# Output projection: one 64-row tile's high and low activations share one stationary tile of 128 columns, and that tile moves from ninth to fifth place

## What is computed

```python
ya = rms_norm(h.astype(dt), g_a) * jax.nn.silu(za)        # first half, 1024 channels
...
yb = rms_norm(ob.astype(dt), g_b) * jax.nn.silu(zb)       # second half, 1024 channels
y = jnp.concatenate([ya, yb], axis=-1) @ w_out            # w_out: 2048 x 1024
x_out = x + gate[:, None] * y
...
y_prompt = rms_norm(xp, g_final)
y_sample = rms_norm(xs, g_final)
```

## Time and profile before

| | us |
|---|---|
| median of 3 runs (lowest, highest) | 1128.11 (1127.08, 1128.51) |
| profiled execution, its own time | 1130.15 |
| its span in the trace | 1128.3 |
| PE busy in the span | 1039.0 (92%) |
| DVE / ACT / POOL busy | 864.4 / 494.7 / 392.2 |
| mean granted TensorE clock | 0.973 |

### The profile page before, as it was taken

One profiled execution on the slowest core, in us unless ns is written; L12 is line 12 of the kernel. 1 busy time (PEld: TensorE's weight loads), 2 busy tenths in 40 slices (PEclk: granted clock), 3 DMA queues, 4 the chain that ended last, 5 costly groups with the idle time before them and its releaser, 6 DMA issues.

```text
span 1128.3 us, 16568 instructions
## 1 busy us (share of the span) xinstructions
PE 1039.0 (92%) x5914; PEld 931.5 (83%) x5914; DVE 864.4 (77%) x1643; ACT 494.7 (44%) x827; POOL 392.2 (35%) x247
## 2 busy tenths in 40 slices
PE   5989888999989998989899996899999999999996
PEld 3679666999989998989899995778878878888873
DVE  1578899999998899999999996677667656444344
ACT  4442565211223676765556324556555534111111
POOL 0223665221112444554545571233331332212120
PEclk9989999999999998989999998999999999999998
DMA  9613010232341022222113632243322336132221
GB/s 298 191 43 80 6 40 1 77 115 77 97 135 47 19 80 80 80 80 74 48 39 97 212 105 71 72 108 94 95 57 66 94 94 232 55 114 94 84 66 56
DMA packets 128281, 100.78 MB, mean 89 GB/s; under 512 B 12177, under 2 KB 119201, under 8 KB 128225
## 3 DMA queue, kind: packets, MB, share of 16 engines
q1 hardware_dynamic: 128224, 100.04, 30.2%
HBM read 74.04 MB, written 25.99 MB: 89 GB/s over the span
## 4 chain that ended last, share of the span: by engine, by line
PE 55%; DVE 25%; issue 14%; ACT 4%; DMA 1%; SPq 1%; POOL 1%; DVEq 0%; ACTq 0%
PE ps L566 15%; PE ps L568 15%; PE ps L567 15%; DVE scores L1994 6%; PE ps L1715 5%; DVE best L1990 4%; DVE y_a L2043 3%; DVE hidden L2038 2%; DVE conv L2016 2%; DVE scores L1954 2%; PE ps L1450 2%; PE ps L1435 1%; DVE mult L2033 1%; DVE mult L2024 1%; DMA x_in<-in_x_prompt 1%
## 5 line engine op out<-in xcount | busy, mean ns | idle before, releaser
L566 PE MATMUL ps<-h_hi,w_hi 128*128 128x364 f32 (+3 forms) x984 | 323.8, 329 | 5.1 <-DVE h_lo L1893 4.1
L567 PE MATMUL ps<-h_lo,w_hi 128*128 128x364 f32 (+3 forms) x984 | 322.8, 328 | 0.0
L568 PE MATMUL ps<-h_hi,w_lo 128*128 128x364 f32 (+3 forms) x984 | 322.5, 328 | 0.0
L888 POOL TENSOR_TENSOR w_lo<-w_raw,w_hi 128x1024 fp32r<-128x1024 f32 (+1 forms) x41 | 107.1, 2613 | 316.9 <-ACT w_hi L1079 316.9
L566 PEld LDWEIGHTS ps<-h_hi,w_hi 128*128 128x128 f32 (+1 forms) x984 | 186.4, 189 | 6.8 <-issue 4.2
L567 PEld LDWEIGHTS ps<-h_lo,w_hi 128*128 128x128 f32 (+1 forms) x984 | 186.5, 190 | 1.2
L568 PEld LDWEIGHTS ps<-h_hi,w_lo 128*128 128x128 f32 (+1 forms) x984 | 186.4, 189 | 0.7
L1994 DVE MATCH_REPLACE8 scores<-best,scores 128x512 f32<-128x512 f32 (+6 forms) x204 | 172.3, 858 | 0.0
L1990 DVE MAX8 best<-scores 128x8 f32<-128x512 f32 (+6 forms) x204 | 162.8, 860 | 1.8
L998 POOL TENSOR_TENSOR y_lo<-y_raw,y_hi 128x1024 fp32r<-128x1024 f32 (+1 forms) x18 | 41.3, 2295 | 142.2 <-ACT y_hi L1352 142.2
L2169 DVE TENSOR_TENSOR pt_lo<-ps,pt_hi 128x512 fp32r<-128x512 f32 (+2 forms) x82 | 53.6, 656 | 45.1 <-ACT pt_hi L1370 44.6
(11 more groups left out here) (246 smaller groups left out, 2121.8 us busy)
## 6 DMA issues: line engine op xcount, KB each, us to landing
w_raw<-in_w_in SPq DMA_DIRECT2D x40, 512.0 KB, 4.7
w_mod_raw<-in_w_mod SPq DMA_DIRECT2D x8, 1024.0 KB, 12.1
y_raw<-y_scratch SPq DMA_DIRECT2D x16, 512.0 KB, 4.3
wo_raw<-in_w_out SPq DMA_DIRECT2D x10, 512.0 KB, 5.1
q_scratch<-stage SPq DMA_DIRECT2D x8, 546.0 KB, 3.6
y_scratch<-y_a SPq DMA_DIRECT2D x8, 546.0 KB, 3.6
zb_scratch<-stage SPq DMA_DIRECT2D x8, 546.0 KB, 4.3
x_in<-in_x_prompt SPq DMA_DIRECT2D x8, 512.0 KB, 8.5
```

Source lines behind the costliest of these rows:

```text
L566: nc.tensor.matmul(out, w_part_hi, x_hi, start=first, stop=False)
L567: nc.tensor.matmul(out, w_part_hi, x_lo, start=False, stop=False)
L568: return nc.tensor.matmul(out, w_part_lo, x_hi, start=False, stop=last)
L888: pool.tensor_tensor(w_lo[:, slot, :, 0:width], w_raw[:, slot, :, 0:width], f32(w_hi[:, slot, :, 0:width]), ALU.subtract).then_inc(w_lo_do ...
```

## The change

A table `OUT_TILES` says which tile stands at which place of the output stage. Places 0 to 3 keep tiles 0 to 3, place 4 takes the sample's tile 8, and places 5 to 8 take prompt tiles 4 to 7. `OUT_ORDER` itself is unchanged, so its first numbers are now places: the sample tile becomes items 6 and 11 (it was items 14 and 17), and the last item is prompt tile 7's second half.

For the sample tile POOL writes the low part not into `y_lo` but into columns 64 to 127 of the same `y_hi` block, whose columns 0 to 63 hold the high part. One matmul with that 128-column stationary block and the high weight gives high x high in PSUM rows 0 to 63 and low x high in rows 64 to 127; a second, with 64 stationary columns, adds high x low weight to rows 0 to 63. Behind both sample items DVE brings rows 64 to 127 over to rows 0 to 63 and adds them (`fold`).

```diff
+OUT_TILES = (0, 1, 2, 3, 8, 4, 5, 6, 7)
+def out_tile(t):
+    return tile_at(OUT_TILES[t])
+def stacked(t):
+    return OUT_TILES[t] == NT - 1
...
             def split_y(e):                                   # POOL
-                rows_ = tile_at(OUT_ORDER[e][0])[1]
+                t = OUT_ORDER[e][0]
+                rows_ = out_tile(t)[1]
+                low = y_hi[:, e % 2, :, rows_:P] if stacked(t) else y_lo[:, e % 2, :, :]
                 pool.wait_ge(y_hi_done, e + 1)
-                pool.tensor_tensor(y_lo[:, e % 2, :, 0:rows_], y_raw[:, e % 2, :, 0:rows_],
+                pool.tensor_tensor(low, y_raw[:, e % 2, :, 0:rows_],
                                    f32(y_hi[:, e % 2, :, 0:rows_]), ALU.subtract).then_inc(y_lo_done, 1)
...
             def out_step_of(e, k):                            # PE
                 for q in range(2):
                     cols = slice(512 * q, 512 * (q + 1))
+                    if stacked(t):
+                        both = ps[:, b + q, :], y_hi[:, e % 2, k, :], wh[:, k, cols]
+                        if k < KT - 1:
+                            nc.tensor.matmul(*both, start=(k == 0), stop=False)
+                        x = nc.tensor.matmul(ps[0:rows_, b + q, :], y_hi[:, e % 2, k, 0:rows_], wl[:, k, cols],
+                                             start=False, stop=False)
+                        if k == KT - 1:
+                            x = nc.tensor.matmul(*both, start=False, stop=True)
+                        continue
                     x = split3(k, y_hi[:, e % 2, k, 0:rows_], y_lo[:, e % 2, k, 0:rows_], wh[:, k, cols], wl[:, k, cols],
                                ps[0:rows_, b + q, :], k == 0, k == KT - 1)
...
             def scale_first(t):                               # DVE
-                V.tensor_scalar(acc[t % 3][r, :], banks(e, r), rstd[r, 1, t:t + 1], None, ALU.mult).then_inc(a_scaled, 1)
+                src = banks(e, r)
+                if stacked(t):
+                    src = fold(e, r, acc[t % 3][r, :], 0)
+                V.tensor_scalar(acc[t % 3][r, :], src, rstd[r, 1, i:i + 1], None, ALU.mult).then_inc(a_scaled, 1)
+
+            def fold(e, r, to, n):
+                V.tensor_copy(to, banks(e, slice(r.stop, P))).then_inc(folded, 1)
+                dve.wait_ge(folded, n + 1)
+                V.tensor_tensor(to, to, banks(e, r), ALU.add).then_inc(folded, 1)
+                dve.wait_ge(folded, n + 2)
+                return to
...
             for t in range(NT):                               # DVE, final steps
-                V.scalar_tensor_tensor(w, banks(e, r), rstd[r, 2, t:t + 1], w, ALU.mult, ALU.add).then_inc(out_step, 1)
+                src = banks(e, r)
+                if t >= 2:
+                    dve.wait_ge(y_out[t % 2], 16 * (t // 2))
+                if stacked(t):
+                    src = fold(e, r, y, 2)
+                V.scalar_tensor_tensor(w, src, rstd[r, 2, i:i + 1], w, ALU.mult, ALU.add).then_inc(out_step, 1)
...
-                if t >= 2:
-                    dve.wait_ge(y_out[t % 2], 16 * (t // 2))
                 V.tensor_tensor(y, w, x_res[r, t % 2, :], ALU.add).then_inc(out_step, 1)
```

More of the change, by code:

```diff
@@ L558, in build @@
     a_scaled = sem("a_scaled")
+    folded = sem("folded")
     out_step = sem("out_step")
@@ L792, in load_y @@
                 t, half = OUT_ORDER[e]
-                t0, rows_ = tile_at(t)
+                t0, rows_ = out_tile(t)
                 if e >= 2:
@@ L828, in load_x @@
             def load_x(t):
-                rows_ = tile_at(t)[1]
+                rows_ = out_tile(t)[1]
                 if t >= 2:
                     sp.wait_ge(out_step, 3 * (t - 1))
-                sp.dma_start(x_res[0:rows_, t % 2, :], row_slice(x_rows, t)).then_inc(xres_in[t % 2], 16)
+                sp.dma_start(x_res[0:rows_, t % 2, :], row_slice(x_rows, OUT_TILES[t])).then_inc(xres_in[t % 2], 16)
             def store_y(t):
-                rows_ = tile_at(t)[1]
+                rows_ = out_tile(t)[1]
                 sp.wait_ge(fin_done, t + 1)
-                sp.dma_start(row_slice(y_rows, t), y_fin[0:rows_, t % 2, :]).then_inc(y_out[t % 2], 16)
+                sp.dma_start(row_slice(y_rows, OUT_TILES[t]), y_fin[0:rows_, t % 2, :]).then_inc(y_out[t % 2], 16)
             def load_wob(k):
@@ L1343, in split_y @@
             def split_y(e):
-                rows_ = tile_at(OUT_ORDER[e][0])[1]
+                rows_ = out_tile(OUT_ORDER[e][0])[1]
                 act.wait_ge(y_in[e % 2], 16 * (e // 2 + 1))
@@ L2127, in scale_first @@
                 e = OUT_ORDER.index((t, 0))
-                r = slice(0, tile_at(t)[1])
+                i = OUT_TILES[t]
+                r = slice(0, tile_at(i)[1])
                 dve.wait_ge(proj_ready, e + 1)
@@ L2209, in _ @@
             for t in range(NT):
-                rows_ = tile_at(t)[1]
+                i = OUT_TILES[t]
+                rows_ = tile_at(i)[1]
                 r = slice(0, rows_)
@@ L2215, in _ @@
                 dve.wait_ge(a_scaled, t + 1)
-                V.scalar_tensor_tensor(w, banks(e, r), rstd[r, 2, t:t + 1], w, ALU.mult, ALU.add).then_inc(out_step, 1)
+                src = banks(e, r)
[4 more added lines that the diff above has]
+                V.scalar_tensor_tensor(w, src, rstd[r, 2, i:i + 1], w, ALU.mult, ALU.add).then_inc(out_step, 1)
                 dve.wait_ge(out_step, 3 * t + 1)
-                V.tensor_tensor(w, w, gate_rows[r, 0 if t < NT - 1 else 1, :], ALU.mult).then_inc(out_step, 1)
+                V.tensor_tensor(w, w, gate_rows[r, 0 if i < NT - 1 else 1, :], ALU.mult).then_inc(out_step, 1)
                 dve.wait_ge(out_step, 3 * t + 2)
                 dve.wait_ge(xres_in[t % 2], 16 * (t // 2 + 1))
-                if t >= 2:
-                    dve.wait_ge(y_out[t % 2], 16 * (t // 2))
                 V.tensor_tensor(y, w, x_res[r, t % 2, :], ALU.add).then_inc(out_step, 1)
```

## The result

The changed kernel took 1123.29 us (median of 5 runs, 1121.48 to 1128.77) beside 1128.19 us (5 runs, 1127.08 to 1129.19) for the kernel before: a ratio of 0.9954, 95% interval 0.9937 to 0.9970. It is faster, by 4.9 us in the medians where 7.4 were forecast, and 0.9 us above the range. The profiled execution took 1123.64 us (1130.15 before), its span is 1121.9 us. One later run, of the kernel with the stacking alone, fell in a slow state (1165.53 us at a granted clock of 0.847) and is left out of that kernel's median.

What follows compares the result with a forecast made beforehand. PE's matmul issue was taken to bound the output stage. 32 fewer matmuls save 7.4 us, with width changes, fold, cover, DMAs and tail at 0: 1128.11 - 7.4 = 1120.7 us, range 1119.4 to 1122.4.

Steps and rivals of the forecast that it cites:

- What bounds the stage: Output stage, last 170 us: matmul issue on PE and nothing else until the last matmul starts, then a serial tail.
- 32 matmuls in place of 48: Each sample item: 64 matmuls at 0.2305 us make 14.75 us in place of 22.12, saving 7.4 us.
- 60 changes of width at 0: Both sample items: switching between 128 and 64 stationary columns, 30 times an item, charged 0; upper bound 9.6 us.
- three borders: Places in the earlier trace where stationary width changes, into items 14 and 17 and out of 14; claimed ordinary pitches.
- The rival with emptied arrays: Sample items: each width change empties the array, 9.6 us lost against 7.4 gained, 1130.3 us; chance 0.03.
- the one with long weight loads showing: Sample items: 52 ns of a long load shows at each of 60 changes, 3.1 us, giving 1123.8; chance 0.05.
- The fold beside PE: DVE behind both sample items: a copy and an add, 2.6 us each time, cost on the path 0.
- The other bound, 7.0 us beside POOL: Fold on DVE: operations reach 3.50 us when POOL works too, so 7.0 each time; even that fits.
- Cover behind the short items: Items 6 and 11: 7.4 us each, next activations ready after 3.8 us, leaving 3.6 us, so PE does not wait.
- The tail: Behind the last matmul: 7.64 us of steps stay with 128 rows; larger store within 0.3 us either way, taken as 0.
- The step that failed: End of the sum: median 2.0 us under the profiled execution, so 1128.11 - 7.4 = 1120.7 us, 0.66% faster.
- the bounds it names: Likeliest case's own range, 1119.4 to 1122.0: saving 7.2 to 7.6, 0.3 for the store, earlier runs' spread.

Runs made afterwards that it cites:

- the second ratio: The changed kernel, unedited, timed again beside the kernel before on chip 3: 1123.2 us (6 runs), ratio 0.9945 (0.9926 to 0.9963).
- the all-wide items: Changed kernel with the stacked items' narrow matmuls taking all 128 stationary columns, so the width never changes: 1122.08 us (4 runs), ratio 0.9937.

## Why the prediction was right and wrong

- *What bounds the stage.* Right: PE without gaps before and after, 132.8 us and 125.4.
- *32 matmuls in place of 48.* Right: 14.81 us for the two items where 14.75 was worked out, 7.3 of 7.4 us saved, half of it in each item.
- *60 changes of width at 0.* Right, and shown by taking them away: 1 ns each at most. (Of the three borders that it names it reads two; the third, into item 17, is 0.23 us as well.) The rival with emptied arrays and the one with long weight loads showing are both out.
- *The fold beside PE.* Right at fifth place: 2.44 us for 2.6, no wait of PE. The 2.6 us in the tail if it had stayed last became 2.8. The other bound, 7.0 us beside POOL, did not fit the fold: its add beside POOL kept 1.21 us, and the step behind it was the one that grew.
- *Cover behind the short items.* Right for this kernel. The slack of 3.6 us leaves 0.2 when 2.4 us of POOL's work is added, since the second subtraction and DVE's addition stretched each other, and the loss beyond it is larger than the overrun, since PE's clock falls.
- *The tail.* 0 was taken between -0.3 and +0.3; it is -0.2 to -0.3. From the store's issue to the end it is 3.2 us with 512 KB and was 3.5 with 256 KB, the difference of the two landings in the earlier trace rows.
- *The step that failed* is the last of the sum, "The median of the runs is 2.0 us under the profiled execution, so 1128.11 - 7.4 = 1120.7 us". Three runs from 1127.08 to 1128.51 were taken as the level of the kernel before and as its spread. In 77 further runs, in sets of 25, 12, 23 and 17, its medians are 1130.18, 1130.58, 1129.78 and 1130.18, and its range is 1125.33 to 1138.91. Nor is a profiled execution 2.0 us above the median as a rule: in the eleven later sets of two or more runs it lay between 0.95 us under and 3.4 over. Taking 7.4 from 1130.18 gives 1122.8, and from the profiled execution's own 1130.15 the same; measured were 1123.29 and 1123.2. So the difference was right and the level was 2 us low. The range was too narrow for a start of the stage that wanders by 9 us; the bounds it names (7.2 and 7.6, 0.3, 1127.08 to 1128.51) add up to 1119.2 to 1121.6 and not to 1119.4 to 1122.0.
- *Why the level read low* stays open. All five runs of the kernel before on the first occasion lie at 1129.19 or under, and only 22 of the 77 later ones do, while the changed kernel took the same on both (1123.29, 1123.2). It can be chance or something of that occasion; the granted clock of those five is not known.
- *The first ratio*, 0.9954, against 0.9934 forecast: the profiled execution of the changed kernel shows 1.1 us of the shortfall as the late load. The other executions have no trace; their mean granted clocks run the same way, 0.980 in the shortest (1121.48) and 0.971 in the longest (1128.77), which doesn't show what lowered the clock. That the changed program has no fixed loss rests on the fourteen starts of item 4, on the time from the first rounding to item 4, which is 86.7 to 86.9 us in either kernel where neither the load nor the clock disturbs it, and on the second ratio, whose interval holds the forecast, while the first one's misses it by 0.0003.

## What to carry to other kernels

In this stage a matmul costs by the columns it moves (0.23 us for 512, with 64 stationary columns or 128), so a stationary tile that fills half of its columns is paid in full: put the second operand part into the free columns, and add the halves elsewhere. The place of the tile matters as much as the stacking where the added work falls: 2.5 us of folding is free in the middle of a matmul-bound stage and costs 2.8 behind its last matmul. And when a time is forecast from a few runs, take the difference from the trace and the level from as many runs as there are; three close ones lay 2 us low here.

## What the runs showed of the hardware

- Two stages of one program differ in how well they repeat. The dense one, at a granted clock of 1.00, repeats to 0.1 us in 132.8; what lies ahead of it wandered by 9 us in 960, in the largest case mostly with the granted clock (0.59 against 0.91 over 20 us).
- After 2.96 us without a matmul PE came back at the 1.2 GHz level, matmuls of 512 columns 0.42 us apart in place of 0.23, and the next item took 1.6 us more; after 1.17 us it came back at full speed.
- In the output stage the DVE operations that stretch beside POOL are those that read two SBUF tiles. In the changed kernel POOL subtracts from 1045.52 to 1047.91; the fold's add (SBUF and PSUM) takes 1.21 us and the step behind it, which now reads two SBUF tiles, 2.16 instead of 1.28:

```profile
1045.58 1.21 DVE L2167 TENSOR_TENSOR y_fin<-y_fin,ps 64x1024 f32<-64x1024 f32 x1
1046.83 2.16 DVE L2259 SCALAR_TENSOR_TENSOR acc<-y_fin,rstd,acc 64x1024 f32<-64x1024 f32 x1
```

The Trainium skill (GPSIMD Engine Reference, 1. Specifications) has contention with DVE instructions that are in a 2-port perf mode or have two SBUF inputs; these rows agree with the second. Two full SBUF tiles are not the only case: in the same trace DVE's product of the 128x128 `ident` with one column of `small` (L2147), 0.28 to 0.29 us alone, takes 1.92 us at 922.07, beside a POOL subtraction that starts at 921.53. No run here tells which property of it does that.
- The pitch of a 128-column matmul is 0.2275 us with the first half of the weight and 0.2331 with the second; the all-wide items kept it (7.28 and 7.47 us for 32), and the mixed ones had 0.230 and 0.233. No run here tells why.
